# Rotary parts of the MLA scores stacked on 64 rows, the chunk mask written by VectorE, one filling quarter moved

## The reference, cut to what matters

```python
q_nope, q_rope = q_mla[..., :MLA_NOPE], rope(q_mla[..., MLA_NOPE:], pos)
k_rope = rope(k_rope, pos)
# mla_attend, MLA_NOPE = 64, MLA_ROPE = 32, CHUNK = 64
s = (q_lat . c_kv + q_rope . k_rope) * MLA_SCALE
visible = (k_pos[None, :] // CHUNK) <= (q_pos[:, None] // CHUNK)
p = softmax(where(visible, s, -inf))
o = p @ c_kv
```

## Time and profile before

| | us |
|---|---|
| median of 3 runs | 1875.72 |
| lowest and highest | 1872.34, 1876.59 |
| the profiled execution, its own time | 1875.13 |
| its span, first to last instruction | 1873.3 |
| PE busy | 1847.7 (99%) |
| DVE, ACT, POOL busy | 911.5, 558.2, 1071.3 |
| mean granted TensorE clock, of full | 0.997 |

### The profile page before, as it was taken

How to read it: one execution, slowest core, us unless ns; L and a number is a source line. 1 busy time by engine, 2 the same in 40 slices (tenths; PEclk the granted TensorE clock), 3 DMA queues, 4 the chain that set the end, 5 groups by cost and what they waited for, 6 DMA issues and landing times.

```text
span 1873.3 us, 33907 instructions
## 1 busy us (share of the span) xinstructions
PE 1847.7 (99%) x14390; PEld 1784.7 (95%) x14390; DVE 911.5 (49%) x1538; ACT 558.2 (30%) x1165; POOL 1071.3 (57%) x994
## 2 busy tenths in 40 slices
PE   9999999999999999999999999999999999999999
PEld 8988888999999999999999998899999999999999
DVE  6666665332655531523556766653327555225143
ACT  4434443102522221202244344431124222112021
POOL 8674624655455555557665844346465555555564
PEclk9999999999999999999999999999999999999999
DMA  5232211324222222222243321123332222222222
GB/s 186 86 103 69 74 41 57 102 80 150 68 91 91 90 82 89 91 84 88 96 147 96 103 75 51 40 69 101 119 111 77 83 90 91 91 85 85 81 91 93
DMA packets 74951, 168.40 MB, mean 90 GB/s; under 512 B 6128, under 2 KB 33904, under 8 KB 74800
## 3 DMA queue, kind: packets, MB, share of 16 engines
q1 hardware_dynamic: 67472, 158.69, 26.0%
q10 hardware_dynamic: 7328, 7.54, 1.2%
HBM read 156.41 MB, written 9.79 MB: 89 GB/s over the span
## 4 chain that ended last, share of the span: by engine, by line
PE 88%; DVE 6%; POOL 3%; ACT 2%; DMA 1%; issue 1%; SPq 0%; DVEq 0%; ACTq 0%; POOLq 0%
PE ps L1524 74%; PE ps L1559 2%; PE ps L1683 2%; POOL wsp L597 2%; PE ps L1641 2%; PE ps L1733 1%; PE ps L1738 1%; DVE xn L1063 1%; DVE xT L1396 1%; DVE R L1063 1%; DVE mix L1393 1%; POOL wsp L591 1%; PE ps L1598 1%; DVE xT L1220 1%; PE ps L1706 1%
## 5 line engine op out<-in xcount | busy, mean ns | idle before, releaser
L1524 PE MATMUL ps<-xn,wsp 128*128 128x272 f32 x7824 | 1006.7, 290 | 8.5 <-POOL wsp L597 4.2
L1524 PEld LDWEIGHTS ps<-xn,wsp 128*128 128x128 f32 x7824 | 989.6, 189 | 13.3 <-issue 8.7
L597 POOL TENSOR_TENSOR wsp<-raw,wsp 128x256 fp32r<-128x256 f32 (+1 forms) x578 | 724.2, 1275 | 22.3
L591 POOL CAST wsp<-raw 128x512 fp32r<-128x512 f32 (+2 forms) x372 | 322.2, 880 | 670.1 <-DMA raw<-in_wstream 572.6
L1524 PE MATMUL ps<-R,wsp 128*128 128x272 f32 x3840 | 486.2, 288 | 0.1
L1524 PEld LDWEIGHTS ps<-R,wsp 128*128 128x128 f32 x3840 | 482.7, 189 | 1.2 <-DVE xT L1092 0.5
L1063 DVE SCALAR_TENSOR_TENSOR R<-ps,R 64x256 fp32r<-64x256 f32 (+8 forms) x232 | 127.8, 561 | 94.6 <-ACT R L665 31.2
L1412 DVE TENSOR_TENSOR mix<-ps,rstd 128x272 f32<-128x272 f32 x88 | 38.8, 441 | 202.5 <-PE ps L1524 192.2
L948 ACT ACTIVATE mix<-vv 128x2 f32<-128x2 f32 x88 | 18.0, 204 | 363.0 <-DVE mix L1414 363.0
L1063 DVE SCALAR_TENSOR_TENSOR R<-mix,R 128x544 fp32r<-128x544 f32 (+1 forms) x82 | 70.9, 865 | 81.9 <-ACT R L969 66.9
L1420 DVE SCALAR_TENSOR_TENSOR ps<-mix,vv,ps 128x546 f32<-128x546 f32 x88 | 69.4, 789 | 55.6 <-ACT ps L957 55.6
(11 more groups left out here) (230 smaller groups left out, 1485.7 us busy)
## 6 DMA issues: line engine op xcount, KB each, us to landing
raw<-in_wstream SPq DMA_DIRECT2D x233, 512.0 KB, 3.7
raw<-in_wstream SPq DMA_DIRECT2D x48, 128.0 KB, 2.6
raw<-in_wstream SPq DMA_DIRECT2D x16, 384.0 KB, 3.1
raw<-in_kc SPq DMA_DIRECT2D x8, 512.0 KB, 3.8
raw<-in_vc SPq DMA_DIRECT2D x8, 512.0 KB, 4.7
xT<-in_x_in SPq DMA_DIRECT2D x8, 272.0 KB, 5.2
out_k_out<-mix ACTq DMA_DIRECT2D x8, 272.0 KB, 3.1
xT<-in_x_in SPq DMA_DIRECT2D x1, 2176.0 KB, 8.2
```

The lines of the kernel that those rows point to most:

```text
L591: ins = nc.gpsimd.tensor_copy(dst[:, 0, f], part[:, f])
L597: ins = nc.gpsimd.tensor_tensor(dst[:, 1, f], part[:, f], dst[:, 0, f].bitcast(F32), ALU.subtract)
L1524: mm = pe.matmul(z[:, h], w[:, x, (k0 + k) * P:(k0 + k + 1) * P], rhs[:, y, k, h * HT:(h + 1) * HT], start=(k == 0 and (x, y) == (0, 0)), ...
```

## The change

The raw rotary parts go, prompt columns alone, into the still unused pairs 2 and 3 of o_sb. SyncE waits for the last of them and moves them with eight DMAs inside SBUF into a new layout of qr, in which the 64 partitions of a head hold its high part above its low part. ml_scores then issues four rotary matmuls in place of six: two with 64 rows (high and low query by the high key) and two with 32 rows (high query by the low key). The two mask matmuls are gone; VectorE writes NEG over the invisible 64x64 corner of each head's block ahead of the maxima and waits for that write. TensorE (step 18) and ScalarE (values' product of pair 2, step 12) wait for the DMAs. The last quota of the first list goes from 3 to 2; the second list holds one quarter more and spreads it anew: steps 22, 26 and 31 have 2 in place of 1, steps 29 and 32 have 1 in place of 2.

```diff
-        qr = carve(Ar, 4 * T, 2, 2, T)
+        qr = carve(Ar, 4 * T, PAIRS, SEQ)
+        qr_raw = o_sb[:, :, 2:4, 0:SEQ]
...
+        QR_MOVES = 16 * 8
...
-                      [4, 4, 4, 3, 3, 3, 4, 4, 3, 4, 4, 4, 3, 2, 3, 2, 3, 3] +
-                      [2, 2, 1, 2, 1, 2, 2, 2, 1, 1, 2, 2, 1, 1, 2, 2, 2, 4, 0])
+                      [4, 4, 4, 3, 3, 3, 4, 4, 3, 4, 4, 4, 3, 2, 3, 2, 3, 2] +
+                      [2, 2, 1, 2, 2, 2, 2, 2, 2, 1, 2, 1, 1, 2, 1, 2, 2, 4, 0])
...
+                    load_to(ST_AT[("gb", 0)])
+                    sp_.wait_ge(S["rope_lo"], 3)
+                    for e in range(2):
+                        for r in range(2):
+                            for x in range(2):
+                                sp_.dma_start(qr[64 * r + 32 * x:64 * r + 32 * x + 32, e:PAIRS:2].bitcast(F32),
+                                              qr_raw[64 * e + 32 * r:64 * e + 32 * r + 32, x].bitcast(F32)).then_inc(pre["qr_in"], 16)
                     load_to(ST_AT[("out", 3)])
...
-                            ac(qr[:, 0, n - 1], rope[0], ACT.Copy).then_inc(S["rope_hi"], 1)
+                            ac(qr_raw[:, 0, n - 1], rope[0][:, 0:SEQ], ACT.Copy).then_inc(S["rope_hi"], 1)
...
+                        if t[0] == "pvas" and t[1] == 2:
+                            act.wait_ge(pre["qr_in"], QR_MOVES * (layer + 1))
...
-                            lo(qr[:, 1, n - 1], rope[0], qr[:, 0, n - 1], "rope_lo")
+                            lo(qr_raw[:, 1, n - 1], rope[0][:, 0:SEQ], qr_raw[:, 0, n - 1], "rope_lo")
...
+                            link(v.memset(z_view(s, P * (qb + 1))[0:CHUNK, :, P * qb + CHUNK:P * (qb + 1)], NEG))
                             link(v.reduce_max(negmax[:, n], z_view(s, P * (qb + 1)), mybir.AxisListType.X))
...
-                            pe.wait_ge(S["rope_lo"], 3)
+                            pe.wait_ge(pre["qr_in"], QR_MOVES * (layer + 1))
...
-                        for i, (x, y) in enumerate(PARTS):
+                        for y in range(2):
                             for r in range(2):
-                                a = 64 * (t % 2) + 32 * r
-                                pe.matmul(z[:, r], qr[a:a + 32, x, t // 2, qb * P:(qb + 1) * P], krT[a:a + 32, y, 0:w],
-                                          start=False, stop=False, tile_position=(a, 0), skip_group_check=True)
-                        for r in range(2):
-                            mm = pe.matmul(z[:, r, qb * P:w], ident_b, masks[:, 2], start=False, stop=True, skip_group_check=True)
+                                a = slice(64 * r, 64 * r + (32 if y else 64))
+                                mm = pe.matmul(z[:, r], qr[a, t, qb * P:(qb + 1) * P], krT[a, y, 0:w],
+                                               start=False, stop=(y == 1), tile_position=(64 * r, 0), skip_group_check=True)
                         mm.then_inc(S["z_done"], 1)
```

More of the change, by code:

```diff
@@ L449, in build @@
             pre = {n: st.enter_context(nc.semaphore(n)) for n in
-                   ("con_in", "late_in", *(f"x_in{k}" for k in range(KT)), "c_in", "half_hi", "half_lo", "y_done0", "y_gate0", "y_raw0", "made", "eps_made", "squares", "added", "summed", "logs", "roots",
+                   ("con_in", "late_in", *(f"x_in{k}" for k in range(KT)), "c_in", "half_hi", "half_lo", "y_done0", "y_gate0", "y_raw0", "qr_in", "made", "eps_made", "squares", "added", "summed", "logs", "roots",
                     "y_st")}
```

## The result

The changed kernel takes 1881.32 us (median; 1876.91 to 1882.94), the kernel before 1873.97 beside it (1871.93 to 1876.59): ratio 1.0034, 95% interval 1.0024 to 1.0044. It is slower by 0.24 to 0.44%, where 1870.4 and faster was forecast. The profiled execution is 1878.92 us, span 1877.1 against 1873.3.

The account below looks back on a forecast made before the run. TensorE, busy 99% of the span, was taken as the bound. Per layer 5.2 us saved less 2.05 of new waits, 6.2 for both: 1875.13 to 1868.9 us, with one clock fall 1870.4; range 1865 to 1876.

Parts of the forecast that it names:

- What leaves TensorE: Score blocks of the second branch: removed rotary and mask matmuls save 5.2 us a layer, 10.4 us in two layers.
- the price of the removed matmuls: Rotary blocks: two of six matmuls go, priced at a third, 0.16 to 0.30 us by width.
- the row measures the pair itself: Rotary block at 512 columns: six matmuls in 0.89 us, so 0.30 us for a removed pair.
- Its move is in the waits alone: Filling quarters: same number in both kernels, so moving them only changes waits, 2.05 us more per layer.
- TensorE's clock: Behind the waits of steps 29 and 30: an even chance in each layer of a clock fall costing 1.5 us.
- between dense blocks: Step 18's wait: like an idle 1.68 us where nothing was lost, so no clock fall forecast there.
- The rival "slower": Clock falls at steps 18 and 30 of both layers, 2.5 us each: +3.8, so 1879 us; chance 0.08.
- step 18's wait: Ahead of step 18's scores, TensorE waits for the low part of unit 16: 1.15 us new per layer.
- step 30's two waits: Behind step 29's single quarter: 0.7 us ahead of the scores, 1.3 us ahead of the transposes.
- the vanished waits of steps 23, 27 and 32: These waits go because steps 22, 26 and 31 now have two quarters.
- the memset: VectorE's write of the mask: 0.2 us with its wait, covered by ScalarE's work; 0 to 0.3 us in effect.
- steps 22, 26 and 30 eat their saving: TensorE comes sooner but waits for the softmax chain: 0.2 us in step 22, 0.45 in 26, 1.3 in 30.

Follow-up runs that it names:

- e1: The changed kernel with both quota lists put back to those of the kernel before; 1867.98 us, ratio to before 0.9970.
- e3: The changed kernel with the moved quarter back in step 17 and one taken from step 22; 1876.52 us, ratio to before 1.0012.
- e5: The changed kernel with the old first list and a second list that never has two single quarters in a row; 1870.70 us, ratio to before 0.9981.
- e11: The changed kernel with the old first list and the second list spread only from step 27 on; 1867.15 us, ratio to before 0.9967.
- e2: The kernel before with both quota lists of the changed kernel; 1884.41 us, ratio to before 1.0054.
- e12: The changed kernel with unread products, eleven ahead of step 18's scores and ten ahead of step 30's transposes; 1874.07 us, ratio to before 1.0005.
- e6: The kernel before with the quota lists of e5; 1875.72 us, ratio to before 1.0006.
- e9: The changed kernel with ten unread products ahead of step 30's transposes; 1876.95 us, ratio to before 1.0017.

## Why the prediction was wrong

The profiled execution was forecast 4.7 us under before (6.2 less 1.5 for one fall) and came 3.8 over: 8.5 to explain.

1. **What leaves TensorE: right in kind, too large.** Forecast 1.28 a head pair, 10.4 in all; measured 0.91, so 7.3. Missing: 3.1 us. The failed term is the price of the removed matmuls, a third of the block of six. Measured in the changed kernel at 512 columns, the four take the 0.80 us between these rows, where 0.59 was forecast:

```profile
216.03 0.97 PE L1745 MATMUL ps<-R,Ar 64*128 64x512 f32 x6
216.84 0.82 PE L1750 MATMUL ps<-R,Ar 64*128 64x512 f32 x4
217.64 0.93 PE L1695 MATMUL ps<-R 128*128 128x512 f32 x3
```

The starts of the single matmuls say why. The two heads' matmuls start 3 ns apart, as a pair. From one pair to the next it takes, in us, as medians over the eight units of a width (at 128 columns the last entry of each row is from step 18, where no wait follows):

| columns | run | nope pairs | rotary pairs | masks |
|---|---|---|---|---|
| 128 | before | 0.165, 0.109, 0.207 | 0.163, 0.113, 0.206 | 0.095 |
| 128 | e1 | 0.162, 0.113, 0.113 | 0.204, 0.255 | |
| 512 | before | 0.338, 0.232, 0.321 | 0.338, 0.228, 0.327 | 0.095 |
| 512 | e1 | 0.338, 0.234, 0.227 | 0.327, 0.425 | |

The middle pair of a block is the cheapest; the last one, ahead of another shape, takes 0.09 to 0.10 us more, and the first one 0.05 to 0.11 more. A third of the block holds its share of both, but the number of changes of shape stayed as it was, and what left is one pair at the middle price: 0.11, 0.12, 0.175 and 0.23 us for the four widths, 0.635 a head pair and 5.1 us in all, where 7.0 was forecast. The 64-row pair does replace the 32-row one at nothing extra, as forecast: both stand ahead of a change of shape and take 0.204 against 0.206 us, and 0.327 against 0.327. The masks' 0.10 us went too, but the first matmul of the block behind now takes 0.02 to 0.05 us longer to the next start, 0.115 a head pair, 0.9 us in all. So "the row measures the pair itself" was wrong: the row held the changes of shape as well. The Trainium skill's page "TensorE: Matmul & The Clock Gate" (Measured speedup vs the span model) has a packed pair cost hardly more than one matmul. By that rule the prediction had estimated 5.0 us for the pairs, and the 5.1 measured agrees with it.
2. **"Its move is in the waits alone": the step that failed outright.** It looked at two semaphores ahead of each step and not at the banks. 1.09 us a layer ahead of the sample values of step 19 and 0.31 ahead of step 33's products, 2.8 us in both layers. That these are due to the banks follows from the end of the copy 0.1 us ahead in step 19, from e1 and e3 without the quarter, and, for the mechanism, from e5 against e11. In step 33 the bank is that of tile ql 3 in both kernels; what is new is the single quarter in step 32 behind it, and again the products start 0.10 us after VectorE's last copy of that tile (292.03 + 0.21):

```profile
292.03 0.21 DVE L1074 SCALAR_TENSOR_TENSOR R<-ps,R 128x64 fp32r<-128x64 f32 x1
292.34 0.93 PE L1695 MATMUL ps<-R 128*128 128x512 f32 x3 [0.30 <-issue]
```

Another bank for these values alone, with the lists kept, wasn't tried.
3. **TensorE's clock: right mechanism, wrong chance and price.** It was to fall in one layer of two at 1.5 us. Behind step 30's pair it fell in six places of six, and in four of them (e2, e3) for 7 to 10 us; e3's in layer 0 cost 4.0 us. At step 18, left out as "between dense blocks", it fell in four of eight places, all four behind waits of 1.38 us or more, never behind the three of 1.03 to 1.08. In the profile of after the falls cost 3.4 us: 1.6 in step 18 of layer 0 (9.05 against e12's 7.46) and 0.9 at each step 30 (branches 104.63 and 103.13 against 102.2). That is 1.9 more than the forecast. The rival "slower" had just these places and the result nearest to the truth, 1879, at a chance of 0.08. That its number is so near is luck: three of its four places fell, for 3.4 us in place of 10, and the rest came from points 1 and 2, which it didn't have.
4. **The weight chunks.** Layer 1's wait of 1.22 was 2.46, and 0.75 came at its start: 2.0 us, of which layer 0 gave back 1.6 in step 10 (shorter wait, shorter half clock) and layer 1 0.15. The first of the two can't be put on the change: e6, which has the old scores and no moves, waits 2.52 there too, and all the other runs 1.9 to 2.5. The 1.22 of the first profile was the exception. The second, at 970.22, may hang on the change: a wait of 0.5 to 1.0 us stands there in ten of the eleven profiles with the new scores (not in e9) and in none of the three with the old ones. No run takes it apart.
5. **Right:** step 18's wait (1.46 and 1.03, forecast 1.15), step 30's two waits, the vanished waits of steps 23, 27 and 32, the wait of 0.36 in step 26 (0.45), the memset at 0.17 us (0.2) and its cover, the moves at nothing on TensorE's branch, and that steps 22, 26 and 30 eat their saving. Step 31's wait of 0.25, forecast to stay, was gone behind the longer step 30.

Points 1 to 3 give 3.1 + 2.8 + 1.9 = 7.8, point 4 some 0.3, step 18's waits 0.2. That is 8.3 of the 8.5; smaller differences of either sign, such as step 31's wait, are left out.

The median lies 2.4 us above the profiled execution. In its seven executions the time goes with the mean granted clock: 0.996 at 1876.91, 0.995 at 1878.92 and 0.994 in the five from 1880.86 to 1882.94. More or longer falls, as e3's, would do that, but no profile shows where they are, so it stays open. Open too is when exactly the clock falls: at step 10, behind the late weight chunk, it fell after 1.22 us of waiting in before and didn't after 2.46 in e1 and e3.

## What to carry to other kernels

Before work is moved from one step to another, list who gets which PSUM bank under the new order, and when its last reader ends; a shift by one step can put a product behind a copy that comes late, and such a wait shows as "issue", not as the name of an engine. Two short waits with only small matmuls between them can cost far more than their length: here 0.9 us (changed kernel) to 4.0 us (e3) came on top of 1.8 us of waiting. Price them with the clock at half behind them, or break them up by giving the step its second quarter. Price a removed matmul by the distance of starts in the middle of its block, not by the block over its count. Split a change like this into its halves first: one gained 6 us and the other lost 10.

## What was not expected of the hardware

- Short idle pieces, 0.59 + 1.20 us within 2.7 us of the timeline (272.29 to 275.00), brought TensorE to half clock each time, and in e3 it stayed there through 9 us of work without a gap (271 to 280). The Trainium skill's page "TensorE: Matmul & The Clock Gate" (A second HAM failure mode: psum-queue depth-cycling) has a case of this kind, an engine that idles briefly but often and whose clock goes up and down; these traces agree, with the granted clock of 0.50 in the rows above.
- Ten products that nobody reads, 1.5 us, in a wait that can't be shortened keep the clock up: the quarter behind took 1.77 us in place of 3.09.
- A pair of fp32 matmuls on separate rows of the array takes 0.11 us at 128 columns and 0.23 at 512 in the middle of a block, and 0.09 to 0.10 us more where matmuls of another shape follow; 64 rows or 32 make no difference there.
- A memset of 64 partitions by 128 elements on PSUM takes 0.17 us on VectorE.
